# Gate rows of a memory layer: spread over the partitions by transfers instead of by TensorE, masked by GpSimd, with their exponentials taken earlier

## What is computed

```
logf = log_sigmoid(f_pre);  bcum = cumsum(logf)
D    = where(causal, bcum[t] - bcum[s] + i[s], -inf)
m    = max(max_s D, bcum + m_before)
Smat = (q k^T) * exp(D - m)
h    = (Smat v) / max(|sum_s Smat|, exp(-m))
```

## Time and profile before

| | |
|---|---|
| median of 3 runs | 981.37 us |
| profiled execution | 981.05 us |
| its span (first to last instruction) | 979.3 us |
| PE busy | 919.2 us (94%) |
| POOL, ACT, DVE busy | 631.7, 541.3, 468.9 us |
| DMA | 139.93 MB, 143 GB/s |

### The profile page before, as it was taken

How to read it: one execution, slowest core, us unless ns; L and a number is a source line. 1 busy time by engine, 2 the same in 40 slices (tenths; PEclk the granted TensorE clock), 3 DMA queues, 4 the chain that set the end, 5 groups by cost and what they waited for, 6 DMA issues and landing times.

```text
span 979.3 us, 24214 instructions
## 1 busy us (share of the span) xinstructions
PE 919.2 (94%) x9548; PEld 874.0 (89%) x9548; DVE 468.9 (48%) x862; ACT 541.3 (55%) x805; POOL 631.7 (65%) x273
## 2 busy tenths in 40 slices
PE   4999999999978789999999999999988999999997
PEld 4988777899978779999999989999877999999996
DVE  5256544785779854433330133574445743333112
ACT  6577664665845876444444347676543655544441
POOL 2886334377797327977777856564513678888882
PEclk9999999999999999999999999999999999999999
DMA  9654123254534305655555543433002445556551
GB/s 348 202 171 151 66 86 103 71 170 133 173 114 147 130 23 172 196 175 176 175 180 173 173 151 129 132 128 108 4 5 89 141 161 194 193 171 194 189 177 44
DMA packets 39046, 139.93 MB, mean 143 GB/s; under 512 B 4272, under 2 KB 5552, under 8 KB 38832
## 3 DMA queue, kind: packets, MB, share of 16 engines
q1 hardware_dynamic: 38960, 138.68, 42.5%
HBM read 137.62 MB, written 1.05 MB: 142 GB/s over the span
## 4 chain that ended last, share of the span: by engine, by line
PE 59%; issue 8%; DVE 8%; POOL 5%; ACT 5%; POOLq 0%; ACTq 0%; DVEq 0%
PE ps L798 59%; POOL wlo L727 5%; ACT ps L1605 1%; ACT whi L1685 1%; DVE wlo L2154 1%; DVE hA L2587 1%; DVE qkl L2154 1%; DVE aL L2163 1%; DVE mad L2154 0%; DVE hT L2190 0%; DVE ps L2154 0%; DVE ivt L2163 0%; POOL dif L751 0%; DVE mad L2374 0%; ACT qkl L1605 0%
## 5 line engine op out<-in xcount | busy, mean ns | idle before, releaser
L727 POOL TENSOR_TENSOR wlo<-ring,whi 128x1024 fp32r<-128x1024 f32 x243 | 584.9, 2422 | 296.1 <-ACT whi L1685 288.5
L1685 ACT ACTIVATE whi<-ring 128x1024 fp32r<-128x1024 f32 x253 | 266.7, 1060 | 207.2 <-PE ps L798 186.5
L798 PE MATMUL ps<-aH,whi 128*128 128x272 f32 (+1 forms) x1048 | 306.1, 292 | 7.3 <-DVE aL L2200 4.9
L798 PE MATMUL ps<-aH,wlo 128*128 128x272 f32 (+1 forms) x1048 | 300.2, 286 | 0.0
L798 PE MATMUL ps<-aL,whi 128*128 128x272 f32 (+1 forms) x1048 | 299.5, 286 | 0.0
L798 PEld LDWEIGHTS ps<-aH,whi 128*128 128x128 f32 x1048 | 198.9, 190 | 12.9 <-DVE wlo L2154 4.8
L798 PEld LDWEIGHTS ps<-aL,whi 128*128 128x128 f32 x1048 | 198.8, 190 | 0.6 <-issue 0.5
L798 PEld LDWEIGHTS ps<-aH,wlo 128*128 128x128 f32 x1048 | 198.8, 190 | 0.0
L798 PE MATMUL ps<-fxH,whi 128*128 128x256 f32 x480 | 135.7, 283 | 3.4 <-DVE fxL L2154 1.8
L798 PE MATMUL ps<-fxL,whi 128*128 128x256 f32 x480 | 135.0, 281 | 0.0
L798 PE MATMUL ps<-fxH,wlo 128*128 128x256 f32 x480 | 135.0, 281 | 0.0
(11 more groups left out here) (382 smaller groups left out, 1324.6 us busy)
## 6 DMA issues: line engine op xcount, KB each, us to landing
ring<-in_stream SPq DMA_DIRECT2D x253, 512.0 KB, 3.3
cst<-in_cst SPq DMA_DIRECT2D x1, 1325.0 KB, 12.9
xT<-in_x SPq DMA_DIRECT2D x4, 272.0 KB, 3.3
out<-hT SPq DMA_DIRECT2D x4, 256.0 KB, 2.3
row<-in_row SPq DMA_DIRECT2D x1, 898.0 KB, 9.1
cst<-in_cst SPq DMA_DIRECT2D x1, 704.0 KB, 10.2
mat<-in_mat SPq DMA_DIRECT2D x1, 576.0 KB, 13.8
vec<-in_vec SPq DMA_DIRECT2D x1, 135.0 KB, 3.6
```

The lines of the kernel that those rows point to most:

```text
L727: nc.gpsimd.tensor_tensor(wlo[:, s, :], ring[:, s, :], whi[:, s, :].bitcast(F32), ALU.subtract).then_inc(S("w_split"), 1)
L798: return nc.tensor.matmul(out, lhsT, rhs, start=start, stop=stop, skip_group_check=True)
L1685: nc.scalar.activation(whi[:, v % SLOTS, :], ring[:, v % SLOTS, :], ACT.Copy).then_inc(S("w_high"), 1)
```

## The change

The two rows of every head are written to a small tensor in the chip's memory by ACT's queue in slot 11 (`rows_out`) and read back, spread over all partitions, by five transfers of ACT's queue in slot 15 (`rows_in`): M of heads 0 and 1 into rs, M of heads 2 and 3 into a free part of mixT, m of all heads into mem. POOL adds the mask to both (two instructions, before the low half of slot 20's unit, `MASK_AT`). ACT takes exp of mem for all heads and of heads 0 and 1 in slot 24, and of heads 2 and 3 in slots 29 and 30 (`gate_powers`). PE's front keeps only q by k. The absolute value of the denominators stays in PSUM, so that DVE's maximum reads PSUM and mem.

```diff
+        rows_d = nc.dram_tensor("gate_rows_d", (4, 2, T), F32).ap()
-        mE = flat_rs[:, 0:768].rearrange("p (w t) -> p w t", w=2)
+        mE = [t[:, 0:768].rearrange("p (w t) -> p w t", w=2) for t in (flat_rs, mixT[:].rearrange("p a b -> p (a b)"))]
...
             pool.wait_ge(S("w_split"), 2)
-            lows(2, U_H + 20)
+            lows(2, even_unit(MASK_AT))
+            pool.wait_ge(S("rows_in"), 80)
+            pool.wait_ge(S("masks"), 4)
+            for i in range(2):
+                e = mE[i].rearrange("p w (b t) -> p w b t", t=P)[:, :, 0::2, :]
+                later = before[:].unsqueeze(1).unsqueeze(1).broadcast_to([P, 2, 2, P])
+                nc.gpsimd.tensor_tensor(e, e, later, ALU.add).then_inc(S("rows_masked"), 1)
+            lows(even_unit(MASK_AT), U_H + 20)
...
             def mlstm_front(h):
                 if h == 0:
-                    pe.wait_ge(S("row_max"), 3)
                     pe.wait_ge(S("qk_ready"), 2)
                     pe.wait_ge(S("att_pt"), 12)
                 else:
                     pe.wait_ge(S("mlstm_st"), h)
-                one = C("pick", 512, 4)[:, h * P:(h + 1) * P]
-                mm(ps[:, 5, 0:T], one, rows4[:, 2, :], True, False)
-                mm(ps[:, 5, 0:P], ident_bf[:], before_bf[:], False, True)
-                mm(ps[:, 5, T:T + P], one, rows4[:, 2, P:T], True, False)
-                mm(ps[:, 5, T:T + P], ident_bf[:], before_bf[:], False, True)
-                mm(ps[:, 4, 0:T], one, rows4[:, 3, :])
...
+                    if j == 24:
+                        act.wait_ge(S("rows_in"), 80)
+                        func(mem[:], mem[:], ACT.Exp, scale=-1.0)
+                        for h in range(2):
+                            gate_powers(h)
...
+            def rows_out():
+                act.wait_ge(S("row_max"), 3)
+                nc.scalar.dma_start(rows_d, rows4[:, 2:4, :]).then_inc(S("rows_out"), 16)
+            def rows_in():
+                act.wait_ge(S("rows_out"), 16)
+                def row(what, h0, n, t0):
+                    return rows_d[h0:h0 + n, what, t0:T].unsqueeze(0).broadcast_to([P, n, T - t0])
+                for i in range(2):
+                    nc.scalar.dma_start(mE[i][:, :, 0:T], row(0, 2 * i, 2, 0)).then_inc(S("rows_in"), 16)
+                    nc.scalar.dma_start(mE[i][:, :, T:T + P], row(0, 2 * i, 2, P)).then_inc(S("rows_in"), 16)
+                nc.scalar.dma_start(mem[:], row(1, 0, 4, 0)).then_inc(S("rows_in"), 16)
+            def gate_powers(h):
+                act.wait_ge(S("rows_masked"), h // 2 + 1)
+                e = mE[h // 2][:, h % 2, :]
+                func(e[:, 0:T], e[:, 0:T], ACT.Exp, scale=-1.0, bias=gl[:, 5, h:h + 1])
+                func(e[:, T:T + P], e[:, T:T + P], ACT.Exp, "mlstm_e", scale=-1.0, bias=gl[:, 5, 4 + h:5 + h])
...
-                    func(mad[:, (m - 1) % 2, :], ps[:, 7, T:2 * T], ACT.Abs, "mlstm_d")
-                if m < 4:
-                    act.wait_ge(S("mlstm_s"), m + 1)
-                    if m >= 2:
-                        act.wait_ge(S("mlstm_st"), m - 1)
-                    func(mem[:, m, :], ps[:, 4, 0:T], ACT.Exp, scale=-1.0)
-                    func(mE[:, m % 2, 0:T], ps[:, 5, 0:T], ACT.Exp, scale=-1.0, bias=gl[:, 5, m:m + 1])
-                    func(mE[:, m % 2, T:T + P], ps[:, 5, T:T + P], ACT.Exp, "mlstm_e", scale=-1.0,
-                         bias=gl[:, 5, 4 + m:5 + m])
+                    func(ps[:, 7, T:2 * T], ps[:, 7, T:2 * T], ACT.Abs, "mlstm_d")
+                if m < 2:
+                    gate_powers(m + 2)
...
-                    tt(d, d, mem[:, m - 1, :], ALU.max)
+                    tt(d, ps[:, 7, T:2 * T], mem[:, m - 1, :], ALU.max)
...
                     dve.wait_ge(S("mlstm_e"), m + 1)
-                    stt(mST[:, m % 2, :], ps[:, 6, 0:384], 0.25 * P ** -0.5, mE[:, m % 2, :], ALU.mult, ALU.mult, "mlstm_st")
+                    dve.wait_ge(S("mlstm_s"), m + 1)
+                    stt(mST[:, m % 2, :], ps[:, 6, 0:384], 0.25 * P ** -0.5, mE[m // 2][:, m % 2, :], ALU.mult, ALU.mult, "mlstm_st")
```

More of the change, by code:

```diff
@@ L97 @@
 MM_BANKS = 4
+MASK_AT = 20
 def chunk_bank(c):
@@ L508, in program @@
         later_bf = sb("later_bf", [P, P], BF16)
-        before_bf = sb("before_bf", [P, P], BF16)
+        before = sb("before", [P, P])
         notyet_bf = sb("notyet_bf", [P, P], BF16)
@@ L1709, in even_in @@
                 between = {3: (masks,), 5: (forget_log,), 8: (queries_sq,), 10: (queries_rs, hidden), 12: (by_feature,),
-                           13: (second_layer, log_table), 14: (kc_rs, gates)}
+                           13: (second_layer, log_table), 14: (kc_rs, gates), 11: (rows_out,), 15: (rows_in,)}
                 for j in range(E_UNITS):
@@ L1771, in masks @@
                 func(ident_bf[:], C("ident"), ACT.Copy, "masks")
-                func(before_bf[:], C("gt"), ACT.Copy, "masks", scale=BIG)
+                func(before[:], C("gt"), ACT.Copy, "masks", scale=BIG)
                 func(notyet_bf[:], C("nge"), ACT.Copy, "masks", scale=BIG)
```

## The result

The changed kernel takes 992.4 us (median; 991.04 to 998.36), the kernel before, beside it on the same chip, 982.0 us. The ratio is 1.0107, 95% interval 1.0085 to 1.0129: 1.1% slower, outside the range of the prediction (976.0 to 985.6). The profiled execution of after is 992.43 us, its span 990.6, its mean granted clock 0.98 (before 0.995).

What follows compares the result with a forecast made beforehand. PE, busy 94% of the span, was taken to bound the kernel, with a second loop right behind it in the memory slots. Terms -7.8 + 2.9 + 4.2 + 1.2 = +0.5 us gave 981.9 us, range 976.0 to 985.6.

Steps and rivals of the forecast that it cites:

- Memory slots, -7.8: Memory heads: rows and masks leave PE, DVE's maximum stops waiting for POOL, slots become 5.45 us; gain 7.8 us.
- rival 3: Memory heads: the maximum still waits for POOL with PSUM input, gain only 2.0; +6.3 us, 987.7; chance 0.06.
- Slot 24, +2.9: Five ACT exponentials stand ahead of a copy PE waits for; +2.9 us (2.6 to 3.1), wait becomes 3.5.
- Chain on pc, +4.2: Slots 15 to 19: late transfers push POOL's work into DVE's products on pc, delaying PE; +4.2 us (-1.3 to 6.7).
- The clock, +1.2: Behind PE's longer wait for pc the granted clock falls once, +1.2 us; none counted for slot 25.
- Cost nothing elsewhere: Rest of the kernel: less POOL idle time and 1.3 MB more traffic add 0 us.
- Rival 2: Transfers land at about 92: pc chain 6.7 us late, clock falls at both waits, 2.4; +4.2, 985.6; chance 0.20.

Runs made afterwards that it cites:

- after_sbuf: The changed kernel with the denominators' absolute values written to SBUF again instead of PSUM; 995.91 us, ratio 1.0128 to the kernel before.
- exps_early: The changed kernel with slot 24's five exponentials put ahead of that slot's high half instead of behind it; 983.89 us, ratio 1.0018 to the kernel before.
- filled: The changed kernel with useless 432-column matmuls, seven in PE's wait for pc and four in its slot 25 wait; 984.90 us, ratio 1.0032 to the kernel before.
- both_even: As both, with five useless 16-column matmuls per memory head in place of the five removed; 981.27 us, ratio 0.9988 to the kernel before.
- early_all: As both, with `rows_in` in slot 13 and eight useless 128-column matmuls in the wait for pc; 982.28 us, ratio 1.0003 to the kernel before.
- early_all10: As early_all, with ten useless 128-column matmuls instead of eight; 976.62 us, ratio 0.9936 to the kernel before.
- in13: The changed kernel with `rows_in` called in slot 13 instead of 15; 989.47 us, ratio 1.0076 to the kernel before.
- both_fill10: As both, with ten useless 128-column matmuls in the wait for pc; 978.19 us, ratio 0.9958 to the kernel before.
- mask24: The changed kernel with POOL's wait for the transfers and two masks moved from before unit 24 to before unit 28; 985.58 us, ratio 1.0030 to the kernel before.
- both: The changed kernel with the masks before unit 28 and slot 24's exponentials ahead of its high half; 981.72 us, ratio 0.9983 to the kernel before.
- both_even_fill: As both_even, with four useless 432-column matmuls in the wait for pc; 980.72 us, ratio 0.9981 to the kernel before.

## Why the prediction was wrong, point by point

- **Memory slots, -7.8:** right. 8.0 measured, backs 5.4 to 5.5 apart, maximum 0.42 (rival 3 is out; after_sbuf shows what a maximum that waits looks like).
- **Slot 24, +2.9:** right. +3.0, and exps_early takes it away.
- **Chain on pc, +4.2:** right in mechanism and nearly in size: +3.6 of waiting matmul for matmul, though the transfers landed at 91.1 and not at 88.5. The chain ended at 101.27 where I had 99.7, 5.7 us later than in before, but PE itself came 2.2 us late to the wait (1.5 of it by the low clock at 91) and so waited less.
- **The clock, +1.2: this step failed.** I counted one fall behind one wait at the 3.4 us of the earlier trace rows, and none for the wait in slot 25. Measured are three low stretches of 3.4, 13.7 and 6.8 us, which cost 1.5 + 3.5 + 2.8 = 7.8 us. The single row that I read the price from lies where the large matmuls of the units follow; behind the waits at 101 and 149 stand 6.6 and 3.5 us of small products first, and the clock stayed low for longer. Whether these products are the reason was not tried. filled shows that it is the standing still of PE that brings the two stretches at the waits, not the transfers' traffic; what brings the one at 91, ahead of them, it doesn't show.
- **"Cost nothing elsewhere": failed too.** Taking 32 records from PE brought a stop of 2.4 us into the small products at 329 us, with a low clock behind it: +2.5, shown by both_even, early_all and early_all10. I read PE's part of the change as time alone and not as a number of instructions.
- +1.7 at 720 to 746 has the same look: short waits on "issue" at records 6583, 6711, 6837, 6965, 7092, 7474 and 7601 in before and after alike, of which number 7474 takes 1.22 us in before and 2.59 in after. Before also has 2.13 us at number 7601, where after has 0.20, and after has 3.4 us of low clock at 752.8. Which part of it is chance between executions was not tried.
- **Rival 2 (0.20)** was the nearest: a late landing (about 92; measured 91.1) and a clock fall at both waits. Both came true. Its price for the two falls, 2.4 us, was as far off as the forecast's, and it knew nothing of the stop; by its sum the time was 985.6.

With the clock at 7.8 and the two late terms the prediction's sum would be 0.5 + 6.6 + 2.5 + 1.7 = +11.3, against +10.4.

Left open: what sets how long the clock stays low (in13 and both_fill10 had more of it than I expected), what the "issue" waits are, and the low stretch of 3.4 us near 90 us, ahead of the first wait. It stands in after and in most versions with the transfers, but not in mask24, both, both_even_fill and early_all10, and a single profiled execution of each can't tell an edit from chance there.

## What to carry to other kernels

A new wait of TensorE can cost its own length and then the lower clock behind it. Read that price from a place where the same kind of work follows, and give it a wide range. Before giving instructions to an engine, look at what stands behind them in its order and where it is idle: five exponentials a few lines higher were worth 5.8 us in the trace. When a change takes instructions off TensorE, look where its "issue" waits fall afterwards. Here a handful of useless instructions in an existing wait did away with such a stop; in filled and early_all10 the clock held up too, in both_fill10 not throughout.

## What the runs showed of the hardware that was not expected

- TensorE's "issue" waits stand at fixed record numbers of the program, 2861 and 2988, then 6583, 6711, 6837, 6965 and 7092, so 126 to 128 records apart, the same in versions of 9516 to 9548 records. In groups of 16-column products they cost 0 to 2.7 us, and two instructions more or fewer, some 220 us earlier, decided between 2.72 us and none (early_all, early_all10).
- The granted clock near 0.5 lasted 3.4, 6.8, 10.2 or 13.7 us at waits of 2.3 to 6.2 us; with useless matmuls in both waits (filled) it stayed at 1.00 behind them, and with ten in the first (both_fill10) it fell 10 us later, for 6.8 us, behind a wait of 1.55 us.
- The five spreading transfers, issued by ACT from 81.4 to 84.1 us (0.40 to 0.64 us each; ACT's next work starts at 84.09, after 1.61 us of idle time), landed 4.7 to 7.5 us after issue, where a ring slot of the weights of like size takes 3.3.
